# Thirty-two expert passes instead of thirty-three: the crowded expert's overflow rides in its own pass, and the combination moves between the up products

## The reference

```python
def moe(x, w_router, b_router, w_up, b_up, w_down, b_down):
    logits = (xf @ w_router + b_router)           # 256 tokens, 32 experts
    top_v, top_i = lax.top_k(logits, TOP_K)       # TOP_K = 4
    w = jax.nn.softmax(top_v, axis=-1)
    ...                                           # tokens sorted by expert
    h = lax.ragged_dot(xs, w_up, sizes) + b_up[sorted_e]      # 1024 -> 2048
    g, lin = jnp.split(h, 2, axis=-1)
    g = jnp.minimum(g, 7.0); lin = jnp.clip(lin, -7.0, 7.0)
    act = g * jax.nn.sigmoid(1.702 * g) * (lin + 1.0)
    y = lax.ragged_dot(act, w_down, sizes) + b_down[sorted_e] # 1024 -> 1024
    ...                                           # times w, summed per token
```

## Time and profile before

| | us |
|---|---|
| median of 3 runs | 1932.92 |
| the profiled execution | 1932.22 |
| its span, first to last instruction | 1930.2 |
| TensorE busy in the span | 1823.0 (94%) |
| VectorE busy | 745.5 (39%) |
| ScalarE busy | 615.4 (32%) |
| mean DMA rate over the span | 307 GB/s |
| mean granted TensorE clock | 0.983 |

### The profile page before, as it was taken

How to read it: one execution, slowest core, us unless ns; L and a number is a source line. 1 busy time by engine, 2 the same in 40 slices (tenths; PEclk the granted TensorE clock), 3 DMA queues, 4 the chain that set the end, 5 groups by cost and what they waited for, 6 DMA issues and landing times.

```text
span 1930.2 us, 29833 instructions
## 1 busy us (share of the span) xinstructions
PE 1823.0 (94%) x12120; PEld 1248.1 (65%) x12120; DVE 745.5 (39%) x1574; ACT 615.4 (32%) x1095; POOL 85.7 (4%) x104
## 2 busy tenths in 40 slices
PE   5999999999999999998999999999999999999997
PEld 4855899999899998868444445444444444444446
DVE  2575677556577645375112112122121121221216
ACT  3456555444455535374111111011011111110115
POOL 0010111000111101001000000000000000000002
PEclk8999999999999999898999999999999999999998
DMA  9638555564465554206999999999999999999991
GB/s 393 250 157 342 224 178 188 183 235 168 179 225 178 194 181 165 88 1 243 375 424 426 425 425 427 425 427 426 425 428 426 426 427 426 426 427 425 427 424 46
DMA packets 64941, 592.80 MB, mean 307 GB/s; under 512 B 6000, under 2 KB 9328, under 8 KB 10448
## 3 DMA queue, kind: packets, MB, share of 16 engines
q1 hardware_dynamic: 64416, 589.75, 75.2%
q10 hardware_dynamic: 432, 1.71, 0.2%
HBM read 590.39 MB, written 1.05 MB: 306 GB/s over the span
## 4 chain that ended last, share of the span: by engine, by line
PE 52%; DMA 28%; DVE 10%; ACT 7%; issue 2%; SPq 1%; ACTq 0%; POOL 0%; DVEq 0%
DMA ring<-in_experts 27%; PE ps L2367 15%; DVE wd_lo L1179 6%; ACT wd_hi L718 4%; PE ps L2377 3%; PE ps L1856 3%; PE ps L1852 3%; PE ps L1853 3%; PE ps L2354 2%; PE ps L2132 2%; PE ps L2127 2%; PE ps L2128 2%; PE ps L1906 2%; PE ps L1870 1%; PE ps L1871 1%
## 5 line engine op out<-in xcount | busy, mean ns | idle before, releaser
L2367 PE MATMUL ps<-ring,A 128*64 128x512 f32 x2112 | 468.6, 597 | 38.8 <-ACT A L1061 22.8
L2367 PEld LDWEIGHTS ps<-ring,A 128*64 128x64 f32 x2112 | 169.0, 137 | 333.6 <-issue 332.8
L1715 DVE TENSOR_TENSOR A<-ps,W 128x512 f32<-128x512 f32 x66 | 45.4, 688 | 788.8 <-PE ps L2404 788.8
L1179 DVE TENSOR_TENSOR wd_lo<-ring,wd_hi 128x2048 fp32r<-128x2048 f32 x107 | 244.7, 2290 | 185.4 <-ACT wd_hi L718 185.4
L1852 PE MATMUL ps<-aL_hi,wd_hi 128*128 128x256 f32 x1040 | 256.8, 285 | 3.7 <-ACT wd_hi L718 2.0
L1853 PE MATMUL ps<-aL_lo,wd_hi 128*128 128x256 f32 x1040 | 254.9, 283 | 0.0
L718 ACT ACTIVATE wd_hi<-ring 128x2048 fp32r<-128x2048 f32 x107 | 203.8, 1905 | 118.2 <-PE ps L2132 69.8
L2377 PE MATMUL ps<-ring,A 128*64 128x512 f32 x1056 | 233.9, 595 | 0.0
L1852 PEld LDWEIGHTS ps<-aL_hi,wd_hi 128*128 128x128 f32 x1040 | 199.3, 192 | 6.5 <-issue 5.2
L1853 PEld LDWEIGHTS ps<-aL_lo,wd_hi 128*128 128x128 f32 x1040 | 199.5, 192 | 0.1
L1050 ACT ACTIVATE A<-ps 128x512 f32<-128x512 f32 x66 | 39.4, 597 | 472.6 <-PE ps L2367 472.6
(11 more groups left out here) (365 smaller groups left out, 2178.9 us busy)
## 6 DMA issues: line engine op xcount, KB each, us to landing
ring<-in_experts SPq DMA_DIRECT2D x198, 2048.0 KB, 17.2
ring<-in_weights SPq DMA_DIRECT2D x161, 1024.0 KB, 5.0
hT<-in_x SPq DMA_DIRECT2D x1, 1024.0 KB, 7.6
hT<-in_ctx SPq DMA_DIRECT2D x1, 1024.0 KB, 15.0
hT<-in_weights SPq DMA_DIRECT2D x1, 1024.0 KB, 5.9
tab<-in_tables ACTq DMA_DIRECT2D x1, 768.0 KB, 10.5
out<-aT SPq DMA_DIRECT2D x2, 384.0 KB, 2.5
A<-in_tables SPq DMA_DIRECT2D x1, 548.0 KB, 6.4
```

The lines of the kernel that those rows point to most:

```text
L1179: dve.tensor_tensor(wd_lo[:, b], cell(PLAN[name]["first"][k]["cell"]), wd_hi[:, b].bitcast(F32), ALU.subtract).then_inc(split_lo, 1)
L1715: dve.tensor_tensor(m_gl[:, j].rearrange("p c h n -> p (c h) n"), ps[:, 6 + j, :].rearrange("p (c n) -> p c n", c=8), b_up[:, bass.ds(e * ...
L2367: mm = pe.matmul(ps[h * CAP:(h + 1) * CAP, 4 + j, :], xg[:, c, :], w[:, c, h], start=(c == 0), stop=(c == KC - 1))
```

## The change

- `PASSES` is 32. An order table (`order`, one int per pass, read by SyncE at the head of each pass) replaces the loop number as the expert. VectorE exchanges the crowded expert with expert 16 in one table `passed` of 21 rows (positions, weights, expert number, up biases) x 32, so that the crowded expert comes in pass 16 (`CROWDED`).
- In pass 16 32 further slots (`EXTRA`) run beside the 64: a wider gather in pass 15 (96 columns), then after each `up` and `down` the same weights once more for 32 tokens, on four column tiles of 32 (`extra_up`, `extra_down`), whose partial sums are added when the result is turned (`extra_turn`, a product with `add_pairs`) and, for the down result, in the combination (`extra_combine`, in pass 17). The cells of the ring are given free after these.
- In every pass the order is now: `up(0)`, combination, transposes of `u` half 0, `up(1)`, `oht`, two chunks of the gather, transposes of half 1, rest of the gather, `down`. Banks: the down result goes to bank 5, the gather to bank 7, the transposes to banks 6 and 4. The wait for `y` at the head of a pass is gone (the combination keeps its own).
- The last pass has no gather. `gate_round(1)` stands behind the copy of `y` in the last pass instead of ahead of it, and VectorE's `gate_split(1)` moves behind the residual additions.
- The further stage runs if an expert has more than 96 tokens, if two have more than 64, or if expert 0 has more than 64.

```diff
-PASSES = NE + SPILL
+CROWDED = 16
+EXTRA = 32
+TURN_BANKS, GATHER_BANK, DOWN_BANK = (6, 4), 7, 5
+PASSES = NE
...
-                with sp.Fori(1, NE) as e:
+                sp.wait_ge(spill_ready, 1)
+                with sp.Fori(1, NE) as p:
+                    e = sp.value_load(order[0:1, bass.ds(p, 1)], min_val=0, max_val=NE - 1)
                     for m in range(MPAIRS):
-                        sp.wait_ge(moe["fed"], e * MCELLS + pair_fed(m) - MCELLS)
+                        sp.wait_ge(moe["fed"], p * MCELLS + pair_fed(m) - MCELLS)
                         load_pair(m, e)
...
+                step(dve.tensor_tensor(swap_tmp, passed[:, :, 0:NE], mine21, ALU.mult))
+                step(dve.tensor_reduce(chosen_row, swap_tmp, AX_X, ALU.add))
+                step(dve.tensor_tensor(swap_tmp, passed[:, :, 0:NE], of_crowded.broadcast_to([P, 21, NE]), ALU.subtract))
+                step(dve.tensor_tensor(swap_tmp, swap_tmp, mine21, ALU.mult))
+                step(dve.tensor_tensor(passed[:, :, 0:NE], passed[:, :, 0:NE], swap_tmp, ALU.subtract))
+                step(dve.tensor_copy(of_crowded.rearrange("p r n -> p (r n)"), chosen_row))
+                dve.tensor_copy(order[:], expert_of).then_inc(spill_ready, 1)
...
+                def quarter(h, c):
+                    t = 2 * h + c % 2
+                    return slice(EXTRA * t, EXTRA * (t + 1))
...
+                def extra_up(j):
+                    w = up_cells(4 * j)
+                    pe.wait_ge(extra_act, EXTRA_ACT["xg"][0])
+                    for c in range(KC):
+                        for h in range(2):
+                            mm = pe.matmul(ps[quarter(h, c), 7, :], xg2[:, c, :], w[:, c, h], start=(c < 2), stop=(c >= KC - 2),
+                                           skip_group_check=True)
+                    mm.then_inc(moe["fed"], 4)
...
+                def extra_down(kh, p):
+                    w = down_cells(8 + 2 * kh)
+                    pe.wait_ge(extra_dve, EXTRA_DVE["act"][kh])
+                    pe.wait_ge(moe["xg"], p + 2)
+                    for c in range(4):
+                        for h in range(2):
+                            mm = pe.matmul(ps[quarter(h, c), 7, :], m_act2[:, 4 * kh + c, :], w[:, c, h],
+                                           start=(kh == 0 and c < 2), stop=(kh == 1 and c >= 2), skip_group_check=True)
+                    mm.then_inc(moe["fed"], 2)
...
                     pe.wait_ge(moe["xg"], since(M, "xg") + p + 1)
-                    pe.wait_ge(moe["y"], since(M, "y") + p + 1)
-                    for j in range(2):
-                        up(j, p)
+                    up(0, p, crowded)
+                    if crowded:
+                        extra_up(0)
...
+                    turn(0, p)
+                    if crowded:
+                        extra_turn(0)
+                    up(1, p, crowded)
...
                     if last:
-                        for k in range(2):
-                            gate_round(k, split_hi)
+                        gate_round(0, split_hi)
+                    elif wide_next:
+                        copy_wide(p + 1)
+                    else:
+                        copy_xg(p + 1)
                     act.wait_ge(moe["fed"], since(M, "fed") + (p + 1) * MCELLS)
-                    act.activation(y, ps[:, 4, :], ACT.Copy).then_inc(moe["y"], 1)
+                    act.activation(y, ps[:, DOWN_BANK, :], ACT.Copy).then_inc(moe["y"], 1)
+                    if crowded:
+                        act.activation(y2, ps[:, 7, :], ACT.Copy).then_inc(extra_act, 1)
+                    if last:
+                        gate_round(1, split_hi)
```

More of the change, by code:

```diff
@@ L1590, in route @@
                 step(dve.memset(pos[:, :, PASSES:PASSES + 1], -1.0))
-                step(dve.memset(left[:, :, NE * LATER:NE * LATER + 1], -1.0))
+                step(dve.tensor_copy(expert_of, table("slot", 0, NE)))
                 dve.wait_ge(root_taken, 2)
@@ L1657, in own @@
                     dve.wait_ge(spill_x, n[0])
-                groups = NE * LATER
-                step(dve.scalar_tensor_tensor(out=key, in0=key, scalar=-1.0, in1=table("slot", 0, groups), op0=ALU.add, op1=ALU.subtract))
-                for r in range(LATER):
-                    step(dve.tensor_scalar(later[:, :, r * NE:(r + 1) * NE], pos[:, :, 0:NE], float(-CAP * (r + 1)), None, ALU.add))
+                of_crowded = passed[:, :, CROWDED:CROWDED + 1]
+                mine21 = mine.unsqueeze(1).broadcast_to([P, 21, NE])
@@ new lines, in spill @@
+                step(dve.scalar_tensor_tensor(out=key, in0=full[:, 0:NE], scalar=-1.0, in1=table("slot", 0, NE), op0=ALU.add, op1=ALU.subtract))
+                step(dve.tensor_reduce(full_sum, full, AX_X, ALU.add))
+                step(dve.tensor_reduce(add_pairs, ident.rearrange("p (h c n) -> p h n c", h=2, c=2), AX_X, ALU.add))
+                own()
+                step(dve.tensor_scalar(key[:, CROWDED:CROWDED + 1], key[:, CROWDED:CROWDED + 1], 100.0, None, ALU.add))
+                step(dve.memset(key[:, 0:1], -1000.0))
@@ new lines, in extra_combine, with turn @@
+                def extra_combine():
+                    pe.wait_ge(extra_act, EXTRA_ACT["y"][0])
+                    for n in range(4):
+                        for h in range(2):
+                            rows, f = slice(h * CAP, (h + 1) * CAP), 4 * h + n
+                            pe.matmul(ps[:, f // 2, (f % 2) * T:(f % 2 + 1) * T], y2[rows, n * P:(n + 1) * P], ohT2[rows, :],
+                                      start=False, stop=True, skip_group_check=True)
+                def turn(j, p):
+                    pe.wait_ge(moe["u"], since(M, "u") + p * 2 + j + 1)
+                    for c in range(4):
+                        mm = pe.transpose(ps[:, TURN_BANKS[j], c * P:(c + 1) * P], u[:, j, c * P:(c + 1) * P], ident)
+                    mm.then_inc(moe["turn"], 1)
```

334 lines of the change are left out of this document (228 added, 106 removed).

## The result

The changed kernel takes 1902.27 us (median, 1901.63 to 1903.02), the kernel before 1931.88 us in the same comparison (1929.16 to 1933.67). The ratio is 0.9847, 95% interval 0.9836 to 0.9859: 1.5% faster. The forecast was 1902.7. The profiled execution took 1903.02, its span is 1900.8; before it was 1932.22 and 1930.2.

A forecast was written before the change was run, and what follows sets the result against it. The prediction took the ring's bytes, 29.5 us a pass, to bound the kernel. 1932.2 - 29.5 + 3.0 - 5.4 + 1.6 + 0.5 = 1902.4 profiled, stated as 1902.7 for the runs' median; likeliest case 1898.5 to 1907.5, range up to 1909.

The forecast's parts named there:

- the stall: Passes 17 to 18: late issues of ring loads starve the DMA, +3.0 us (1 to 5).
- ScalarE's rounding: Last pass: two gate roundings instead of one between `y` and the first `aL_hi`, +1.6 us (0 to 1.9).
- half clock term: Before the gate product: TensorE's longer pause, possibly a longer stretch at half clock behind it, +0.5 us (0 to 1.7).
- The pass that goes, -29.5: Expert ring: 33 passes of 12.58 MB become 32, -29.5 us; the stream's start doesn't move, `spill_ready` near 919, cost 0.
- Extra work on TensorE, 13.7 and 1.9: TensorE: extra products and related work take 13.7 us in pass 16, `extra_combine` 1.9 us in pass 17.
- one tile after another: Rival, pass 16: the extra products take 41.2 us instead of 10.3, so 1934, no change; chance 0.02.
- Catching up, 1.6 us a pass: After pass 17: without the wait for `y` TensorE regains 1.6 us a pass; 14 passes wipe out a lag of 12.
- Table read, 0: SyncE's read of `order` at each pass head lies between pair 5's issue and `fed` of `up(0)`: cost 0.
- Tail, -5.4: Last pass after its pair 3: TensorE takes 15.3 us instead of 20.8, -5.4 us.
- Two tiles: Rival, pass 16: extra products run two tiles at a time, 20.6 us, 10.3 later, starving the DMA: 1913; chance 0.08.
- The lag: Rival: a new wait replaces that for `y`, TensorE regains 0.2 us a pass, some 8 us stay: 1911; chance 0.06.
- SyncE's read: Rival, between issues of pairs 5 and 0: the read starves the queue, 1963 at 2.0 us excess a pass; slower 0.02.

The follow-up runs named there:

- The 33rd pass: The changed kernel with a 33rd, empty pass that loads expert 0's weights once more for no token: 1931.53 us, ratio 0.9998.
- fewer bytes: The changed kernel with only half of pair 5 loaded from pass 1 on, one twelfth of the bytes less: 1876.12 us, ratio 0.9707.
- the five executions: Changed kernel, its repeat, and variants with both gate roundings first, 33rd pass, hoisted flag read, identical up to there: whole dents 4.6, 4.6, 4.6, 4.4, 6.3 us.
- `aL_hi` 1.6 us earlier: The changed kernel with both gate roundings ahead of the copy of `y` in the last pass, as in the kernel before: 1902.78 us, ratio 0.9845.
- the two traces without it: Changed kernel with `need_more` read before the last pass and third gate rounding behind the `aL_hi`: 1900.28 us; the same plus the extra combination in pass 24: 1899.81 us.

## Why the prediction was right, and where it wasn't

The gain has the cause that I gave, the bytes of one pass. That the time came out within 0.4 us is partly luck. On the profiled executions the stall came out 1.4 us above its term and ScalarE's rounding 1.5 below; the half clock term was 0.4 too high, and the start of the stream lay 0.8 later in that execution. These happen to cancel.

Two slips stand in the working. 1902.4 and 0.7 are 1903.1, not 1902.7, and 20.8 - 15.3 is 5.5, not 5.4. Neither changes what the runs say.

- **The pass that goes, -29.5: right.** The 33rd pass brings back 29.3 us, and with fewer bytes the kernel gets faster. `spill_ready` fell at 916.55, where I had 919: an operation over 672 columns takes 0.86 us, not 1.33. It stands well ahead of the first free cell.

The swap on VectorE in the changed kernel:

```profile
914.55 0.86 DVE L1738 TENSOR_TENSOR A<-A 128x672 f32<-128x672 f32 x1
915.44 0.86 DVE L1740 TENSOR_TENSOR W<-W,A 128x672 f32<-128x672 f32 x1
...
916.55 0.18 DVE L1744 CAST order<-W 128x32 int32<-128x32 f32 x1
```

- **Extra work on TensorE, 13.7 and 1.9: right.** Pass 16 is 41.29 - 27.70 = 13.6 us longer. The 32 instructions on four column tiles take 3.57 us, 0.11 each; the row carried over, and one tile after another (0.43 each) is ruled out with two at a time. The Trainium skill, TensorE: Matmul & The Clock Gate, Part 3, has 3.07 times for four row tiles; an estimate by it is 4.5 us for 32. The trace has 3.57 us, close to four times, for column tiles in a long run. The 0.16 us for a change of shape doesn't follow from the earlier trace rows, where the 0.43 comes from the same 7.02 us. The chain of waits of the changed kernel has it more directly: the 32 instructions of `up` take 6.87 us behind `down`, which has the same shape (at 1457.03), and 7.02 behind another shape (at 1466.41), so 0.15.
- **The stall, 3.0 (1 to 5): mis-sized, 4.4.** The timing of `fed` was right to 0.3 us: I had L+38.8 and L+50.4 for pass 17's ups, and the trace has the loads behind them issued at L+38.9 and L+50.2, with L = 1395.75. By my limits of 7.6 us before the landing that is 3.7 of stall. I took 3 because the latency might lie under bytes still queued; the traces don't bear that out. The step that failed is "an issue up to 7.6 us before the nominal landing certainly costs nothing", which treats a restart as one late landing. In the changed kernel pair 0 of pass 18 lands 7.6 us after its issue, as expected, but pair 1, issued 0.5 us behind it, lands 6.2 us behind it instead of 4.92. Pair 4 of pass 17, issued 7.9 us before its nominal landing, lost 0 to 1.7 us in the five executions; pair 2 of pass 17, issued 9.5 us before, lost nothing in any. So 7.6 us is too little for a single load and 9.5 was enough here, and a loss behind the late landings comes on top: the term should have been 4 to 6.
- **Catching up, 1.6 us a pass: right.** It is 1.8, and the lateness is gone at pass 22.
- **Table read, 0: right.** The issues stand 29.52 us apart.
- **Tail, -5.4: right.** -5.35; the copy of `u` waits 0.32, I had 0.4.
- **ScalarE's second rounding behind `y`, +1.6: failed, 0.1.** ScalarE did come later (`aL_hi` 4.21 us after the end of `down`, where it was 2.95; I had 4.5). The step that failed is taking ScalarE for the one on which TensorE's pause depends: the gate product starts 4.65 us after the combination in the kernel before and 4.72 in the changed one, and with `aL_hi` 1.6 us earlier it still starts 4.79 after. The read of `need_more` is a part of that pause (0.2 to 1.2 us by the two traces without it); what makes up the rest stays open. The profile before showed that `aL_lo` isn't what the product waits for, had I compared its end with the product's start. The half clock term (+0.5) came out at 0.15.
- **The rivals.** Two tiles is shown false by the timeline, and its price right by experiment. The lag doesn't stay: TensorE waits for the DMA again from pass 22 on. SyncE's read doesn't starve the queue, and no further stage ran.

## What to carry to other kernels

When a stage is bound by its bytes, extra work of another engine is free up to a reserve that the depth of the ring sets. Well past it each microsecond is paid in full (10.3 more cost 10.4 here); near it the account is rougher (3.6 less shortened the stall by 1.3). Work the reserve out issue by issue, as here, and keep about one whole load queued, since a load that restarts the queue lands late and the one behind it can too. Where a wait names an engine whose result was complete long before, the cause lies elsewhere: compare the end of the named instruction with the start of the waiter before pricing anything on that path. A wait removed from a stage bound by something else returns nothing until that stage is late. And look at a second trace before crediting an edit with a microsecond: the 1.6 us behind the gate product did not come again with the same edit.

## What the runs showed of the hardware

- Four column tiles of 32 run four at once in float32, 32 instructions of 512 columns in 3.57 us, shape changes included; on two tiles the same take 7.0.
- A queue of 2.1 MB loads that runs low loses more than the missing time: the same load in the same program landed 7.6 to 10.2 us after its issue, and the load behind it 6.0 to 6.4 us later, for bytes that take 4.92. The Trainium skill, DMA: Bandwidth & Descriptors, Anatomy of one DMA — SWDGE (gpsimd) path, gives about 2.0 us of fixed cost above the bytes. The page measured it on the gpsimd path; an estimate by it puts the landing 6.8 us after the issue. The 7.6 of an empty queue is near that, the 10.2 is not.
- With the flag read from memory ahead of the last pass instead of between two products, TensorE's pause between them was 1.72 and 2.28 us, where it was 2.51 to 2.88 in eleven traces with the read in its old place.
- The clock behind the start of the gate product differed between executions of like programs: a mean of 0.79 over the first 8 us in some, 1.00 in others.
